# Second block of a fused two-block layer stack: the order of its opening steps on ScalarE and VectorE, the place of one memset, and how far ahead the gates' weights are split

## What is computed

```python
h = _rmsnorm(x, norm_g[l])
z = h @ w_in[l]
(nsa_q, nsa_kv, nsa_gate, nsa_silu, fox_qkv, fox_f, fox_silu,
 mem_q, mem_silu, merge_g) = _split(z, IN_SPLITS)
o_a = _nsa(nsa_q, nsa_kv, nsa_gate, ...) * jax.nn.silu(nsa_silu)
o_b = _fox(fox_qkv, fox_f, ...) * jax.nn.silu(fox_silu)
o_m = _memory_xattn(mem_q, mem_kv, ...) * jax.nn.silu(mem_silu)
g = jax.nn.sigmoid(merge_g).reshape(B, T, 3, D)
u = g[:, :, 0] * (o_a @ w_branch_a[l]) + g[:, :, 1] * (o_b @ w_branch_b[l]) + g[:, :, 2] * (o_m @ w_branch_m[l])
x = x + u @ w_out[l]

# in _fox: the forget gate enters the scores as a running sum over the tokens
log_f = jax.nn.log_sigmoid(f_logit + f_bias)
c = jnp.cumsum(log_f, axis=1).transpose(0, 2, 1)
s = einsum(q, k) * scale + cq[..., None] - c[:, :, None, :]
```

## Time and profile before

| | |
|---|---|
| three runs | 3265.39, 3262.95, 3263.2 us (median 3263.2) |
| the profiled execution, its own time | 3262.69 us |
| its span from first to last instruction | 3260.8 us |
| TensorE busy | 3137.0 us, 96% |
| VectorE busy | 1886.1 us, 58% |
| ScalarE busy | 1394.3 us, 43% |
| mean granted TensorE clock | 0.993 |

### The profile page before, as it was taken

How to read it: one execution, slowest core, us unless ns; L and a number is a source line. 1 busy time by engine, 2 the same in 40 slices (tenths; PEclk the granted TensorE clock), 3 DMA queues, 4 the chain that set the end, 5 groups by cost and what they waited for, 6 DMA issues and landing times.

```text
span 3260.8 us, 59864 instructions
## 1 busy us (share of the span) xinstructions
PE 3137.0 (96%) x25752; PEld 2483.0 (76%) x25752; DVE 1886.1 (58%) x3058; ACT 1394.3 (43%) x2454; POOL 446.7 (14%) x440
## 2 busy tenths in 40 slices
PE   8899999999999999999999999999999999999999
PEld 5687778888876687878888876777788767676887
DVE  6576657756466675656745565554444555635443
ACT  5645224434246544334433355454433454544432
POOL 0051430000000331600000002211200011203010
PEclk9899999999999999999999999999999999999999
DMA  5001103333332011123333232222132232221323
GB/s 177 27 22 47 41 29 123 106 95 97 95 116 81 21 29 54 41 71 112 97 97 96 88 122 99 62 65 72 56 94 74 89 109 69 65 72 58 86 73 100
DMA packets 80215, 255.02 MB, mean 78 GB/s; under 512 B 11344, under 2 KB 13008, under 8 KB 78928
## 3 DMA queue, kind: packets, MB, share of 16 engines
q1 hardware_dynamic: 79952, 251.19, 25.0%
HBM read 238.08 MB, written 6.29 MB: 75 GB/s over the span
## 4 chain that ended last, share of the span: by engine, by line
PE 79%; DVE 9%; ACT 6%; issue 2%; DMA 1%; POOL 1%; SPq 1%; ACTq 0%; DVEq 0%; POOLq 0%
PE psum L535 76%; PE psum L700 3%; DVE s_wlo L1971 2%; DVE s_xb L1971 1%; ACT s_tmp L1273 1%; ACT s_whi L1273 1%; DVE s_tmp L1974 1%; DVE s_ffy L1974 1%; DMA s_stage<-w 1%; POOL s_xb L2690 1%; ACT s_E L1273 1%; ACT L1283 1%; SPq L2838 0%; DVE psum L1971 0%; ACT L1273 0%
## 5 line engine op out<-in xcount | busy, mean ns | idle before, releaser
L535 PE MATMUL psum<-s_h,s_whi 128*128 128x512 f32 (+1 forms) x4576 | 1456.9, 400 | 21.2 <-DVE s_wlo L1971 14.3
L535 PEld LDWEIGHTS psum<-s_h,s_whi 128*128 128x128 f32 (+1 forms) x4576 | 847.2, 189 | 235.2 <-issue 34.8
L535 PE MATMUL psum<-s_h,s_wlo 128*128 128x512 f32 (+1 forms) x2288 | 897.5, 392 | 0.0
L1971 DVE TENSOR_TENSOR s_wlo<-s_stage,s_whi 128x1024 fp32r<-128x1024 f32 (+2 forms) x468 | 533.9, 1143 | 358.5 <-ACT s_whi L1273 357.4
L1273 ACT ACTIVATE s_whi<-s_stage 128x1024 fp32r<-128x1024 f32 (+2 forms) x468 | 450.6, 967 | 261.5 <-DMA s_stage<-w 75.9
L535 PEld LDWEIGHTS psum<-s_h,s_wlo 128*128 128x128 f32 (+1 forms) x2288 | 430.8, 188 | 95.1
L2690 POOL TENSOR_TENSOR s_xb<-s_xb,s_cstm 64x512 f32<-64x512 f32 x64 | 101.1, 1579 | 900.5 <-DVE s_xb L1971 896.3
L535 PE MATMUL psum<-s_ffa,s_whi 128*128 128x512 f32 x704 | 217.5, 390 | 4.6 <-DVE s_ffa L1971 4.6
L1974 DVE SCALAR_TENSOR_TENSOR s_ffy<-psum,s_pcol,s_ffy 128x511 f32<-128x511 f32 x176 | 131.7, 748 | 110.8 <-ACT s_ffy L1273 107.7
L1273 ACT ACTIVATE s_E<-psum,s_nm 128x256 f32<-128x256 f32 (+3 forms) x224 | 114.4, 515 | 186.7 <-DVE s_nm L2057 151.3
L535 PE MATMUL psum<-s_oR,s_whi 128*128 128x512 f32 (+1 forms) x640 | 183.4, 371 | 0.0
(11 more groups left out here) (310 smaller groups left out, 4348.2 us busy)
## 6 DMA issues: line engine op xcount, KB each, us to landing
s_stage<-w SPq DMA_DIRECT2D x192, 512.0 KB, 3.6
s_stage<-wup SPq DMA_DIRECT2D x88, 512.0 KB, 3.6
s_stage<-wo SPq DMA_DIRECT2D x32, 512.0 KB, 3.6
s_stage<-wdn SPq DMA_DIRECT2D x32, 512.0 KB, 3.5
s_stage<-wdn SPq DMA_DIRECT2D x16, 384.0 KB, 3.1
spill<-s_x SPq DMA_DIRECT2D x2, 2048.0 KB, 8.7
s_stage<-woa SPq DMA_DIRECT2D x16, 256.0 KB, 2.6
s_x<-spill SPq DMA_DIRECT2D x2, 2048.0 KB, 8.0
```

The costliest lines, as they stand in the source:

```text
L535: return self.e.matmul(out, left, right, start=first, stop=last, skip_group_check=True)
L1971: return self.e.tensor_tensor(out, a, b, op)
```

## The change

On ScalarE and VectorE the two arguments of `together` change places, in both; on TensorE they stay. The memset of `s_crow` moves from the fifth step of `forgetting` to its second. The gates of the first branch and the first merge gates (`silu_gate` with s = 0, `merge_gates`) call `ahead` with 2 tiles beyond, not 1. TensorE's, SyncE's and GpSimd's programs keep their order; no instruction is added or dropped.

```diff
@@ Scalar.layer2 and Vector.layer2
-        together(self.forgetting(l), behind(first, rest, 10, LAG))
+        together(behind(first, rest, 10, LAG), self.forgetting(l))
@@ Scalar.silu_gate and Vector.silu_gate
-            self.ahead(key, 1 if s == 0 else AHEAD)
+            self.ahead(key)
@@ Scalar.merge_gates
-            self.ahead(key, 1)
+            self.ahead(key)
@@ Vector.merge_gates
-            self.ahead((("B", l), "mg", 0, c), 1)
+            self.ahead((("B", l), "mg", 0, c))
@@ Vector.forgetting
         self.e.memset(m.lf[:, :, :], 0.0).then_inc(*self.up("vec_dn", key, "z0"))
+        self.e.memset(m.crow[:, :].bitcast(F32), 0.0).then_inc(*self.up("vec_dn", key, "cz"))
         self.w.wait_ge(*self.at("act_dn", key, 2))
...
         yield
         yield
-        self.e.memset(m.crow[:, :].bitcast(F32), 0.0).then_inc(*self.up("vec_dn", key, "cz"))
         self.w.wait_ge(*self.at("act_dn", key, "crow"))
```

## The result

The changed kernel took 3275.5 us (median of 6 runs, 3272.9 to 3284.9) against 3264.1 of the kernel before on the same chip (3260.5 to 3266.6): a ratio of 1.0041, 95% interval 1.0029 to 1.0053, some 13 us slower. The forecast was 3263.2 in 3256 to 3272. So the kernel lies outside the range, on the slower side. The profiled execution has a span of 3273.6 us, 12.8 more than before.

The account below looks back on a forecast made before the run. TensorE, busy 96% of the span, was taken as the bound. Gone 20.6 us against new 21.3, less about 0.5, gave net +0.2 on 3262.69; with the median 0.5 above, the forecast was 3263.2 us, range 3256 to 3272.

Parts of the forecast that it names:

- hole before the transposes: TensorE stands still before the transposes of `gf`, waiting for its late scaling and copy: 8.2 and 6.7 us.
- one resumption fewer: One restart of TensorE fewer in each layer, giving back about 0.5 us.
- Memset earlier, splits ahead, gates two ahead: From `gf`'s transposes to the second score, waits before k1, s1, s2 and their clock loss go: at most -9.3 and -11.3 us.
- The scaling and copy of `gf` behind q0's work: VectorE scales `gf` only after q0's result, so the transposes start later: 8.2 us idle in the first layer, 6.7 in the second.
- The clock after the hole: TensorE's clock falls after the idle time before the transposes: 2.4 us per layer, 4.8 for both, ends 0 and 3.4 per layer.
- The running sum: TensorE's `s_step` waits for VectorE's late copy of eight columns: 0.8 us per layer, 1.6 for both, bounds 0 and 1.8.
- These three waits I therefore cost at nothing: Split weights for k1, s1 and s2 reach TensorE in time despite the row waiting for v0's transposes: 0 us.
- One new wait appears: Behind the hole the only new TensorE wait is the running sum's, for VectorE's copy: 0.8 us per layer.
- I cost it at 0, between 0 and +1 us per layer: In the attention stretch some seven gate splits come one call earlier, their loads issued 4 us or more before.
- The rival of late split weights: c0's and s2's splits over 3 us later than walked, s2's wait and clock fall remain: +12, 3275 us; chance 0.06.
- The blocking rival: VectorE is blocked, not stretched, beside GpSimd; running sum waits some 4.5 us more per layer: +9, 3272 us; chance 0.08.

Follow-up runs that it names:

- mixed_turns: Kernel before with `s_crow` cleared early, s0 to s3's weights two ahead, and projections' step first in the second turn only; ratio 0.9968 to the kernel before.
- gates_only: Kernel before with only all gates' weights split two ahead, turns in the old order; ratio 0.9988 to the kernel before.
- loads_first: The whole change, with SyncE issuing one more weight load ahead of the second head pair's swap; ratio 1.0009 to the kernel before.
- gf_first: The whole change, but in the first turn the forget gate's step (scaling and copy of `gf`) goes first; ratio 1.0031 to the kernel before.
- tensor_too: The whole change, with TensorE also taking its turns in the new order, projections' step first; ratio 0.9965 to the kernel before.

## Why the prediction was wrong

| term, us, both layers | predicted | measured |
|---|---|---|
| gone: waits for `s_wlo` and their clock | -20.6 | -20.6, all gone |
| hole before the transposes | 8.2 + 6.7 | 9.02 + 6.63 |
| lower clock behind the hole | 4.8 | 2.3 + 2.5 |
| lower clock behind s1's wait | 0 | 1.3 + 0 |
| running sum | 0.8 + 0.8 | 1.15 + 1.05 |
| row's bank before s1 | 0 | 2.10 + 2.10 |
| attention, merge gates' splits | 0, at most +1 per layer | 2.4 + 4.6 |
| one resumption fewer | -0.5 | in the rest |
| sum | +0.2 | +14.6 |

The clock is the busy time above that of an unhindered stretch: 53.14 less 49.5, and 51.81 less 49.3 (mixed_turns has 49.50 us at a granted clock of 1.00 there, first layer). Of the first layer's 3.6 us, 2.3 lie between the transposes and q1's sum of squares: 8.32 us (1939.86 to 1948.18) against 5.97 in the earlier trace rows. The attention's entries are the growth of the stretch from the second score to `s_cPT`: in the first layer 100.30 against 97.87, in the second 102.65 against 98.03, where the scores after the wait also ran at the lower clock (1.56 us for the row at 2743.31 against 1.13). The sum is near the +15.3 of the stretch; the rest of the span was 2.5 us shorter.

*Memset earlier, splits ahead, gates two ahead.* Right: all three waits went.

*The scaling and copy of `gf` behind q0's work.* Right in mechanism and near in size: q0's result, then the scaling of `gf` at 1938.41, its copy at 1939.13, the transposes at 1939.86. That q0's result came at 1937.80 where 1937.7 was walked is luck, since this execution was 0.70 us ahead at q0's first product. Counted from there it was due at 36.3 us and came at 37.1, and that is the 0.8 us by which the first layer's hole is over. The four pieces of q0's swap, behind which k0's weights are loaded, were issued over 3.4 us (1917.03 to 1920.43) instead of 2.4 (1920.38 to 1922.80), and the load took 3.85 us to land instead of 3.63. In the second layer the transposes were due 36.8 us after q0's first product and came there.

```profile
1937.80 0.69 DVE L1974 SCALAR_TENSOR_TENSOR s_q<-s_U,s_cPT 128x512 f32<-128x512 f32 x1 [0.72 <-ACT s_cPT L1273]
1938.41 0.68 DVE L1971 TENSOR_TENSOR psum<-psum,s_rr 32x512 f32<-32x512 f32 x1
```

*The clock after the hole.* 4.8 against 4.8: the granted clock was 0.50 from 1939.86 to 1945.00 and from 2622.04 to 2627.00. Another 1.3 us came behind the wait before s1 in the first layer (1.05 us for the row at 1983.91, against 0.62), which belongs to the first failed step.

*The running sum.* 2.2 against 1.6, within the ends. The late copy and GpSimd as its reason were right; the operations were not stretched but blocked (last section).

*"These three waits I therefore cost at nothing"*, with "One new wait appears". Here the first step failed. The row was seen to be held for the transposes of v0, and the late splits of c0 and s2 behind it were walked; they were indeed in time. What the row itself holds was not asked: the bank of the running sum, which TensorE takes for s1. It cost 4.2 us of waiting and 1.3 us of clock, where the sum had nothing.

*"I cost it at 0, between 0 and +1 us per layer"*, of the gates' weights in the attention stretch. The second failed step, and the larger one: 7.0 us. "The loads they need are issued 4 us or more before the new place, by a narrow margin in one or two": for one split of each layer the load is issued *after* ScalarE stands at it, by 1.75 us in the first layer (2054.12 against 2052.37) and 2.69 in the second (2735.96 against 2733.27). It stands behind a swap for which SyncE waits on VectorE, so its place in time can't be read off the loads' spacing. gates_only and loads_first show this term by itself and gone.

*The rivals.* The rival of late split weights had the right sign and, with 3275, the time, but by luck, since its mechanism did not happen: no split was late. The blocking rival (0.08) was right about what happens and wrong about its price: VectorE did sit out GpSimd's instructions, and the running sum waited 1.15 and 1.05 us, not 4.5 more than 0.8. The 0.06 was too little for a side on which the margins were called narrow. The sum as written gives 3263.4, not 3263.2 (3262.69 + 0.2 + 0.5), which changes nothing.

The two missed terms are one kind of error: at two places I checked that a moved step's *inputs* were there, and not what it keeps from others while it waits.

## What to carry to other kernels

When steps of one chain are moved on some engines, move them on all that take part, or count what each engine's unmoved program expects at each link. A single hole that is explained and then removed may only uncover the next link (gf_first); a cause is shown when all of them go at once (tensor_too). And when a wait is moved, list what the waiting instruction holds, a bank, a buffer or its queue, and for a load look at which queue entry it stands behind rather than at how far apart loads usually are.

## What was not expected of the hardware

VectorE beside GpSimd's squares, first layer of the changed kernel; VectorE's rows, then GpSimd's.

```profile
1952.19 1.16 DVE L2524 TENSOR_SCALAR s_g<-s_g 128x96 f32<-128x96 f32 x1 [0.79 <-ACT s_g L1273]
1953.27 0.18 DVE L1971 TENSOR_TENSOR s_g<-psum,s_prow 128x32 f32<-128x32 f32 x1
1953.43 0.19 DVE L2527 MEMSET s_otok<- 128x160 f32 x1
1955.82 0.97 DVE L1974 SCALAR_TENSOR_TENSOR s_otok<-s_g,s_otok 128x32 f32<-128x32 f32 x1 [1.66 <-ACT s_otok L1273]
...
1957.91 1.79 DVE L1971 TENSOR_TENSOR s_U<-s_U,s_rope 128x512 f32<-128x512 f32 x1
1959.62 1.78 DVE L1971 TENSOR_TENSOR s_tmp<-s_tmp,s_rope 128x512 f32<-128x512 f32 x1
...
1951.39 1.90 POOL L2690 TENSOR_TENSOR s_otok<-s_mkT 128x1024 f32<-128x1024 f32 x1 [529.59 <-DMA s_mv<-memT]
1953.24 1.04 POOL L2690 TENSOR_TENSOR s_otok<-s_mv 128x512 f32<-128x512 f32 x1
...
1955.70 1.04 POOL L2690 TENSOR_TENSOR s_otok<-s_mv 128x512 f32<-128x512 f32 x1
1956.82 4.03 POOL L2690 TENSOR_TENSOR s_otok<-s_otok 128x512 f32<-128x512 f32 x2
```

The operation on 128 x 96 took 0.21 us in the kernel before, at 1941.46 and so ahead of the squares, and takes 1.16 here; it ends at 1953.35, GpSimd's instruction at 1953.29. The one on 128 x 32 took 0.19 there and takes 0.97 here; it ends at 1956.79, GpSimd's at 1956.74. In between, an operation with one input from PSUM (0.18 us) and two memsets (0.19 and 0.48) run at full speed beside GpSimd's. Long operations are caught as well: the two of 128 x 512, 0.69 us by themselves, take 1.79 and 1.78. GpSimd's last two instructions (one row above; 2.33 and 1.63 us) end at 1959.15 and 1960.86, and these two at 1959.70 and 1961.40, 0.55 and 0.54 us later, about what such an operation needs alone. So they are not slowed by a factor, they sit out GpSimd's instruction, and the row's duration contains the waiting: the missing idle time, which I had taken as an open question, says nothing. The Trainium skill, page "SBUF — State Buffer", section "Who interferes with whom", states just this (two SBUF inputs wait, one input doesn't, and a `tensor_scalar` can be caught as well), and the trace agrees. The running sum waited 1.15 us for all this together, where the rival built on blocking had 4.5 more than 0.8. The price is not small by rule: in gf_first, where TensorE comes to the running sum sooner, the same blocking delays its input by 4.2 and 5.3 us, and it waits 3.28 and 6.00.
